# The opening of a two-block transformer kernel: filters, modulation, pooling and the first norm interleaved

## The reference, cut to what matters

```python
# first block
mod = silu(c) @ mod_w + mod_b             # 1024 -> 6 * 1024: sh1, sc1, g1, sh2, sc2, g2
hx = x * (1 + sc1) + sh1
p_g = centred_window_mean(hx_g, w) - hx_g # four groups of 256 channels, w = 2, 4, 8, 16
ox = (p_g @ pool_w_g) * pool_scale
x = layer_norm(ALPHA * x + g1 * ox, ...)
x = layer_norm(ALPHA * x + g2 * swiglu(x * (1 + sc2) + sh2), ...)
# second block: attention, FFN, and a long convolution whose filters come from a small sine network
h = sin(f * (z @ fw1 + b1)); h = sin(f * (h @ fw2 + b2)); h = sin(f * (h @ fw3 + b3))
filters = (h @ fw_out) * decay            # 2 orders, 2 directions, 1024 channels, 512 times
spectra = odd-frequency transform of their sums (cosine) and differences (sine)
```

## Time and profile before

| | |
|---|---|
| runs | 2045.27, 2048.11, 2051.75 us |
| profiled execution | 2047.33 us, span 2046.0 us |
| granted TensorE clock, mean | 0.932 of full speed |
| busy in the span | PE 1814.6 us (89%), DVE 1034.5 (51%), POOL 754.6 (37%), ACT 619.1 (30%) |
| moved | 193.97 MB, 95 GB/s in the mean |

### The profile page before, as it was taken

One profiled execution on the slowest core, in us unless ns is written; L12 is line 12 of the kernel. 1 busy time (PEld: TensorE's weight loads), 2 busy tenths in 40 slices (PEclk: granted clock), 3 DMA queues, 4 the chain that ended last, 5 costly groups with the idle time before them and its releaser, 6 DMA issues.

```text
span 2046.0 us, 19678 instructions
## 1 busy us (share of the span) xinstructions
PE 1814.6 (89%) x7816; PEld 1446.5 (71%) x7816; DVE 1034.5 (51%) x1494; ACT 619.1 (30%) x866; POOL 754.6 (37%) x348
## 2 busy tenths in 40 slices
PE   3882899999998899989999998999566889999997
PEld 1552688888877566768888886787555768888885
DVE  6998533332144758364444224523999464444224
ACT  1222322222224444243333213322222243333212
POOL 3123244444442310234444443342544324444442
PEclk9885799999998999989999998999778989999998
DMA  5771122323222100113232222422111312322232
GB/s 214 269 286 56 37 93 94 102 93 99 97 82 69 62 32 32 62 56 99 93 103 93 93 94 82 154 93 83 62 41 42 114 62 93 99 97 94 95 100 73
DMA packets 48148, 193.97 MB, mean 95 GB/s; under 512 B 5655, under 2 KB 5975, under 8 KB 43384
## 3 DMA queue, kind: packets, MB, share of 16 engines
q1 hardware_dynamic: 47480, 188.52, 27.2%
q10 hardware_dynamic: 576, 4.19, 0.5%
HBM read 180.11 MB, written 12.58 MB: 94 GB/s over the span
## 4 chain that ended last, share of the span: by engine, by line
PE 73%; DVE 19%; ACT 3%; POOL 2%; issue 2%; DMA 1%; ACTq 0%; SPq 0%; DVEq 0%
PE ps L414 23%; PE ps L415 23%; PE ps L416 23%; DVE mod_sums L1345 3%; POOL w_lo L1155 2%; PE ps L525 1%; DVE x_residual L1752 1%; DVE n_values L1477 1%; DVE filter_taps L1328 1%; DVE act_lo L1482 1%; PE ps L730 1%; DVE x_residual L1742 1%; ACT w_hi L854 1%; DVE x_residual L1744 1%; DVE hy_product_lo L1756 1%
## 5 line engine op out<-in xcount | busy, mean ns | idle before, releaser
L1155 POOL TENSOR_TENSOR w_lo<-w_raw,w_hi 128x1024 fp32r<-128x1024 f32 x258 | 621.9, 2411 | 984.7 <-ACT w_hi L854 984.7
L414 PE MATMUL ps<-act_hi,w_hi 128*128 128x512 f32 x1428 | 573.8, 402 | 74.0 <-POOL act_lo L1213 35.8
L415 PE MATMUL ps<-act_lo,w_hi 128*128 128x512 f32 x1428 | 566.9, 397 | 0.0
L416 PE MATMUL ps<-act_hi,w_lo 128*128 128x512 f32 x1428 | 566.0, 396 | 0.0
L854 ACT ACTIVATE w_hi<-w_raw 128x1024 fp32r<-128x1024 f32 x258 | 273.3, 1059 | 747.0 <-PE ps L416 736.1
L414 PEld LDWEIGHTS ps<-act_hi,w_hi 128*128 128x128 f32 x1428 | 274.4, 192 | 148.8 <-issue 51.4
L416 PEld LDWEIGHTS ps<-act_hi,w_lo 128*128 128x128 f32 x1428 | 274.8, 192 | 58.8
L415 PEld LDWEIGHTS ps<-act_lo,w_hi 128*128 128x128 f32 x1428 | 275.5, 193 | 56.3 <-issue 0.5
L414 PE MATMUL ps<-f_hidden_hi,w_hi 128*128 128x512 f32 x528 | 208.0, 394 | 1.9 <-POOL w_lo L1155 1.9
L415 PE MATMUL ps<-f_hidden_lo,w_hi 128*128 128x512 f32 x528 | 206.9, 392 | 0.0
L416 PE MATMUL ps<-f_hidden_hi,w_lo 128*128 128x512 f32 x528 | 206.6, 391 | 0.0
(11 more groups left out here) (263 smaller groups left out, 2296.6 us busy)
## 6 DMA issues: line engine op xcount, KB each, us to landing
w_raw<-in_w_stream SPq DMA_DIRECT2D x258, 512.0 KB, 3.7
mod_ring<-in_mod_w SPq DMA_DIRECT2D x16, 1536.0 KB, 10.2
hy_filter<-spectra SPq DMA_DIRECT2D x8, 1024.0 KB, 4.8
spectra<-filter_spectra SPq DMA_DIRECT2D x4, 1024.0 KB, 9.6
spectra<-filter_spectra ACTq DMA_DIRECT2D x4, 1024.0 KB, 7.4
decay<-in_decay SPq DMA_DIRECT2D x1, 2048.0 KB, 13.6
x_residual<-in_xT SPq DMA_DIRECT2D x8, 256.0 KB, 10.4
x_spill<-x_residual SPq DMA_DIRECT2D x8, 256.0 KB, 10.0
```

The source lines that it names most:

```text
L414: PE.matmul(o, lh, rh, start=start, stop=False, **kw)
L415: PE.matmul(o, lh, rl, start=False, stop=False, **kw)
L416: return PE.matmul(o, ll, rh, start=False, stop=stop, **kw)
L1155: GP.tensor_tensor(B.WL[:, c % 2, :], B.WR[:, c % 2, :], f32(B.WH[:, c % 2, :]), ALU.subtract).then_inc(S.w_lo, 1)
```

## The change

The four functions ahead of the first FFN become one, `start`, in each program, in which everything hangs on the eight filter units.

- Modulation in 48 tiles of 128x1024 (512 KB). Tiles 0 to 11 come with the input channels on the partitions, and PE makes each a column with eight fp32 products, four tiles before the second layer of the sine network, four before the third, four before the first taps. Tiles 12 to 47 come with the output channels on the partitions, and DVE multiplies each by a row of silu(c) and sums in one instruction, six tiles per unit. Four rings of 2, 5, 3 and 7 slots share seven buffers, four of which hold x in token order in between.
- Taps get four banks of their own hand-over: each tile has its own count of taps, decays, high and low parts. All low parts of the taps are POOL's. The order of the units becomes half, order, kind, and half of the decay table is loaded at a time.
- Pooling: PE multiplies x in token order with band matrices of 128x144 (unit 1), DVE forms the difference to hx before it is scaled by ALPHA, the linears come in units 2 and 3 in two banks, the mean in unit 4, the squares in unit 5, the inverse rows after unit 6, and the butterflies of unit 7 amid the normalisation.
- Spectra are stored after each unit from SP's queue. The loads of `fw_out`, the tables, the decay, x and the bands go to ACT's queue. The third and fourth chunk (up_1's base and base+1) are fetched after unit 4.

Buffers, new functions that only rename, and the host's layout are left out below.

```diff
+        own, shared = [self.MW[:, i, :] for i in range(3)], [self.x_tok[:, i, :] for i in range(4)]
+        self.mod_slots = (own[:2], own[2:] + shared, own, own + shared)
...
+MOD_ORDER = (1, 0, 2, 3, 4, 5)
+MOD_PE = 12
+MOD_BATCHES = (12, 18, 24, 30, 36, 42, 46, 48, 48)
+MOD_SLOTS = (2, 5, 3, 7)
+MOD_RINGS = (0, 12, 18, 24, 48)
+MOD_READS = (16, 24, 40, 48)
+MOD_COLUMN = 16
+BAND = P + 2 * PAD
+BAND_AT = (0, P - PAD, 2 * P - PAD, T - BAND)
+BAND_KIND = (0, 1, 1, 2)
+TAP_ORDER = (2, 3, 0, 1)
...
+def mod_place(t):
+    ring = sum(t >= first for first in MOD_RINGS[1:])
+    uses, slot = divmod(t - MOD_RINGS[ring], MOD_SLOTS[ring])
+    return ring, slot, uses
...
+    def mod_tiles(low, high):
+        for t in range(low, high):
+            ring, slot, uses = mod_place(t)
+            PE.wait_ge(S.mod_in[ring][slot], 16 * (uses + 1))
+            at = MOD_COLUMN + t
+            for k in range(KD):
+                ins = PE.matmul(ps[:, 7, at:at + 1], B.mod_slots[ring][slot][:, k * P:(k + 1) * P], B.sc[:, k:k + 1],
+                                start=(k == 0), stop=(k == KD - 1))
+            ins.then_inc(S.mod_pe, 1)
...
+    def taps(v):
+        n, order, kind = unit_parts(v)
+        for at, q in enumerate(TAP_ORDER):
+            if v:
+                PE.wait_ge(S.decayed, 4 * v - 3 + at)
+            PE.matmul(ps[:, q, :], B.hidn[:, q * P:(q + 1) * P], B.fsd[:, kind, order, n * 512:(n + 1) * 512],
+                      start=True, stop=True).then_inc(S.taps, 1)
...
+    def pool_windows():
+        PE.wait_ge(S.x_tok_in, 16)
+        PE.wait_ge(S.band_in, 16)
+        PE.wait_ge(S.mod_read, 1)
+        for k in range(KD):
+            if k == 1:
+                PE.wait_ge(S.odd_copied, 4)
+            if k >= 2:
+                PE.wait_ge(S.diff, k - 1)
+            for s in range(4):
+                ins = PE.matmul(ps[:, POOL_BANKS[k], BAND_AT[s]:BAND_AT[s] + BAND], B.x_tok[:, s, k * P:(k + 1) * P],
+                                B.band[:, 4 * BAND_KIND[s] + k // 2, :], start=(s == 0), stop=(s == 3),
+                                skip_group_check=True)
+            ins.then_inc(S.pooled, 1)
...
+    def pool_linear(cc, v):
+        wh, wl = chunk(cc)
+        for m in range(4):
+            tile = 4 * cc + m
+            if m < 2:
+                PE.wait_ge(S.diff, 8)
+                PE.wait_ge(S.odd_copied, 2 * v + 2)
+                if cc:
+                    PE.wait_ge(S.x_ready, 3 + m)
+            else:
+                PE.wait_ge(S.x_ready, tile - 1)
+            for k in range(2):
+                a = 2 * (m // 2) + k
+                PE.wait_ge(S.diff_lo, 4 * cc + a + 1)
...
+        PE.wait_ge(S.silu_c, 1)
+        mod_tiles(0, 4)
+        PE.wait_ge(S.consts_made, 5)
         for layer in range(2):
             PE.wait_ge(S.hid, layer + 1)
             PE.matmul(ps[0:HY_W, 0, :], B.fws[:, layer * HY_W:(layer + 1) * HY_W], B.hidn[0:HY_W, :],
                       start=True, stop=True).then_inc(S.mlp, 1)
...
+            mod_tiles(4 + 4 * layer, 8 + 4 * layer)
         PE.wait_ge(S.hid, 3)
-        PE.wait_ge(S.fw_sums, 2)
-        PE.wait_ge(S.consts_made, 5)
+        PE.wait_ge(S.fw_sums, 4)
         taps(0)
         for v in range(8):
             if v < 7:
                 taps(v + 1)
-            transforms(v)
-            mod_sum(2 * v)
...
+            for group in range(4):
+                if group == 0:
+                    if v == 2:
+                        PE.wait_ge(S.diff, 8)
+                    elif v in (3, 4):
+                        PE.wait_ge(S.x_ready, 4 * v - 8)
+                    elif v == 6:
+                        PE.wait_ge(S.ln_stat, 1)
+                transform(v, group)
+            if v == 1:
+                pool_windows()
+            elif v in (2, 3):
+                pool_linear(v - 2, v)
+            elif v == 4:
+                first_norm_mean()
+            elif v == 5:
+                first_norm_squares(v)
+            elif v == 6:
+                PE.wait_ge(S.decayed, 32)
+                inverse_rows_of(0, 3)
...
+        def filter_hi(v):
+            for at, q in enumerate(TAP_ORDER):
+                SC.wait_ge(S.decayed, 4 * v + at + 1)
+                if v:
+                    SC.wait_ge(S.spectrum, 4 * v - (1 if q < 2 else 0))
+                SC.activation(B.flh[:, q, :], B.flt[:, q, :], ACT.Copy).then_inc(S.flt_hi, 1)
+        def odd_part(v, f):
+            SC.wait_ge(S.spectrum, 4 * v + (1, 4)[f])
+            if v:
+                SC.wait_ge(S.bfly, 4 * v)
+            SC.activation(B.odd[:, f, :], ps[:, 5, :], ACT.Copy).then_inc(S.odd_copied, 1)
+        def pool_parts(cc):
+            for a in range(4):
+                k = 4 * cc + a
+                if cc == 0:
+                    SC.wait_ge(S.diff, k + 1)
+                    SC.activation(B.hx[:, k, :], B.hx[:, k, :], ACT.Identity,
+                                  bias=B.MOD[:, k:k + 1]).then_inc(S.diff_whole, 1)
+                else:
+                    SC.wait_ge(S.w_used, 1)
+                SC.wait_ge(S.diff_whole, k + 1)
+                SC.activation(AH[:, a, :], B.hx[:, k, :], ACT.Copy).then_inc(S.diff_hi, 1)
         for v in range(8):
-            for q in range(4):
-                SC.wait_ge(S.decayed, 4 * v + q + 1)
...
+            filter_hi(v)
+            if v == 1:
+                SC.wait_ge(S.x_in, 16 * KD)
+                SC.wait_ge(S.affine, 1)
+                SC.wait_ge(S.fw_sums, 4)
+                for k in range(KD):
+                    SC.activation(B.hx[:, k, :], X[:, k, :], ACT.Identity, bias=B.MOD[:, k:k + 1],
+                                  scale=B.AFF[:, 0, 0, k:k + 1]).then_inc(S.pool_in, 1)
+            odd_part(v, 0)
+            odd_part(v, 1)
+            if v == 1:
+                pool_parts(0)
+                for k in range(4, KD):
+                    SC.wait_ge(S.diff, k + 1)
+                    SC.activation(B.hx[:, k, :], B.hx[:, k, :], ACT.Identity,
+                                  bias=B.MOD[:, k:k + 1]).then_inc(S.diff_whole, 1)
+            elif v == 2:
+                for k in range(KD):
+                    SC.activation(X[:, k, :], X[:, k, :], ACT.Copy, scale=ALPHA_1).then_inc(S.x_scaled, 1)
+                pool_parts(1)
+            elif v == 4:
+                w_hi(2)
+                w_hi(3)
+            elif v == 5:
+                for k in range(KD):
+                    SC.wait_ge(S.ln_centred, k + 1)
+                    SC.activation(B.sq[:, k, :] if k < 4 else B.val[:, k, :], X[:, k, :],
+                                  ACT.Square).then_inc(S.ln_square, 1)
...
+        def filter_lo(v):
+            for at, q in enumerate(TAP_ORDER):
+                GP.wait_ge(S.flt_hi, 4 * v + at + 1)
+                GP.tensor_tensor(B.fll[:, q, :], B.flt[:, q, :], f32(B.flh[:, q, :]),
+                                 ALU.subtract).then_inc(S.flt_lo, 1)
+        def pool_lo(cc):
+            for a in range(4):
+                k = 4 * cc + a
+                GP.wait_ge(S.diff_hi, k + 1)
+                GP.tensor_tensor(B.AL[:, a, :], B.hx[:, k, :], f32(B.AH[:, a, :]),
+                                 ALU.subtract).then_inc(S.diff_lo, 1)
+        w_lo(0)
+        w_lo(1)
         for v in range(8):
-            for q in (0, 2):
-                GP.wait_ge(S.flt_hi, 4 * v + q + 1)
...
+            filter_lo(v)
+            if v in (1, 2):
+                pool_lo(v - 1)
+            elif v == 4:
+                w_lo(2)
+                w_lo(3)
+            elif v == 6:
+                norm(0)
...
+        def mod_tile(t):
+            m = 8 * MOD_ORDER[t // 8] + t % 8
+            ring, slot, uses = mod_place(t)
+            src = B.mod_slots[ring][slot]
+            VE.wait_ge(S.mod_in[ring][slot], 16 * (uses + 1))
+            VE.tensor_tensor_reduce(out=src, in0=src, in1=B.c_row[:, :], scale=1.0, scalar=0.0, op0=ALU.mult,
+                                    op1=ALU.add, accum_out=B.MOD[:, m:m + 1]).then_inc(S.mod_dve, 1)
...
+        decays(0)
+        mod_columns()
+        for v in range(7):
+            low, high = MOD_BATCHES[v], MOD_BATCHES[v + 1]
+            middle = min(low + 3, high)
+            mod_tiles(low, middle)
+            decays(v + 1)
+            mod_tiles(middle, high)
+            butterfly(v)
...
+            if v == 1:
+                for k in range(KD):
+                    VE.wait_ge(S.pooled, k + 1)
+                    VE.wait_ge(S.pool_in, k + 1)
+                    VE.scalar_tensor_tensor(out=B.hx[:, k, :], in0=ps[:, POOL_BANKS[k], :],
+                                            scalar=AFF[:, 0, 0, k:k + 1], in1=B.hx[:, k, :], op0=ALU.mult,
+                                            op1=ALU.subtract).then_inc(S.diff, 1)
+            elif v in (2, 3):
+                cc = v - 2
+                for m in range(4 * cc, 4 * cc + 4):
+                    if m % 4 == 3:
+                        VE.wait_ge(S.w_used, cc + 1)
+                    else:
```

(99 more changed lines are left out.)

462 lines of the change are left out of this document (132 added, 330 removed).

## The result

The changed kernel is slower: its runs have a median of 2071.8 us against 2049.93 us for the kernel before on the same chip, a ratio of 1.0086 (95% interval 1.005 to 1.0122). The forecast of 2021 us and its range up to 2048 us missed. The profiled execution took 2063.99 us for a span of 2062.7 us. Two of the four runs lie at 2064 us and two at 2079 us, with a granted clock of 0.942 and 0.934; I compare the profiled executions, which for both kernels are of the shorter kind, and the median holds some 8 us more.

A forecast was written before the change was run, and what follows sets the result against it. The opening was taken as bound by DVE, the 1793.1 us behind it as PE-busy and unchanged. The terms put the first plain linear at 226.1 instead of 252.9 us, 26.8 us less: forecast 2021 us, 8-in-10 range 1992 to 2048.

The forecast's parts named there:

- head, to the first decays: Start of the kernel with PE's twelve modulation tiles: first decays at 46.5 us, bounds 40 and 56.
- first decays, columns, unit 0: First decays and column copy 3 us, then the first filter unit 24 us, 10 of them a new wait.
- unit 1: Second filter unit, six modulation tiles on DVE: 15 us, before the band products.
- band products: Pooling products on PE in the second filter unit, 0.4 us each: DVE stands or works for 11 us.
- unit 4, mean: Fifth filter unit 15 us, then the mean on PE and centring on DVE, 10.6 us.
- unit 5: Sixth filter unit, with only four modulation tiles: 12 us, the squares counted apart at 10 us.
- unit 6: Seventh filter unit, with only two modulation tiles: 9 us.
- tail: From the seventh unit's butterflies to the first plain linear, with the last unit and normalisation: 28 us.
- Head starves: Rival, chance 0.05: twelve tiles through two slots at 5 us each, first taps at 62 rather than 46, 2036 us.
- The tile at twice the price: Rival, chance 0.13: DVE's multiply-and-reduce takes twice 1.25 us in 36 instructions, 45 us more, 2066 us.
- Contention with POOL: Filter units: DVE's two-input instructions wait for POOL, three waits of 0.8 to 1 us, making a unit 15 us.
- The rest: Everything from the first plain linear to the end: 1793.1 us, carried over unchanged.

The follow-up runs named there:

- a2_warm: The changed kernel with 24 unused fp32 products of 128 columns on PE ahead of the first modulation tile: 2077.92 us in one run.
- a4_dve_head: The changed kernel with all 48 modulation tiles on DVE, none on PE, and a first ring of seven slots: 2045.6 us median, ratio 0.9975.
- a1_small_first: The changed kernel with the bulk loads on ACT's queue waiting until the small tensors have landed: 2073.04 us median, ratio 1.0102.
- a3_fetch_early: The changed kernel with weight chunks 0 and 1 fetched behind modulation tile 11 instead of tile 19: 2056.73 us median, ratio 1.0033.
- a6: The changed kernel with the edits of a1_small_first, a3_fetch_early, a4_dve_head and a5 together: 2023.03 us median, ratio 0.9869.
- a8: The changed kernel with two of the four taps' low parts per unit given back to DVE in units 0 to 6: 2072.58 us, ratio 1.008.
- a7: The kernel of a6 with two of the four taps' low parts per unit given back to DVE in units 0 to 6: 2027.08 us median, ratio 0.9861.
- a5: The changed kernel with the high and low parts of chunks 2 and 3 made in unit 6, later than before: 2064.98 us in one run.

## Why the prediction was wrong

The sum was 226.1 us for the start of the first plain linear; it is 265.4. Term by term, measured less predicted:

| step | predicted | measured | error |
|---|---|---|---|
| head, to the first decays | 46.5 | 68.3 | +21.8 |
| first decays, columns, unit 0 | 27 | 31.5 | +4.5 |
| unit 1 | 15 | 18.6 | +3.6 |
| band products | 11 | 9.7 | -1.3 |
| units 2 and 3, linears | 42 | 43.3 | +1.3 |
| unit 4, mean | 25.6 | 19.9 | -5.7 |
| unit 5 | 12 | 18.2 | +6.2 |
| squares | 10 | 10.8 | +0.8 |
| unit 6 | 9 | 13.3 | +4.3 |
| tail | 28 | 31.7 | +3.7 |

**The step that failed** is the head: "2.0 us a tile ... partly at half clock ..., which is 2.9 a tile" and "I let the first land at about 10 us". The tile takes 3.47 us, the first starts at 17.39, and the twelve with two small layers between them and 3 us of waits end at 66.0. That is 68.3 against an upper bound of 56, more than half of the whole error, and by itself it turns 27 us of gain into 5. Of its 21.8 us 7.4 are the late first tile, 12.6 the twelve tiles with what stands between them (the two small layers take 3.8 us on PE, which I had put in the shadow), and 1.8 the first taps. The price of 1.50 us for six products came from a stretch in which PE had just worked on the transforms, and the pooling stretch showed a clock of 0.54 where PE did little. The bound of such a tile is 8 x 0.25 x 2 = 4.0 us, not 2.9, and the measured 3.47 lies between. The record of the clock could not warn me, for it reads 1.00 in the head of the kernel before too, but the durations there could:
```profile
4.22 1.96 PE L447 MATMUL ps<-positions_features,fw 33*64 33x512 f32 x2 [4.22 <-DMA fw_bias_freq<-in_hy_small]
43.49 3.70 PE L459 MATMUL ps<-fw_out_sum_diff,filter_hidden 128*128 128x512 f32 x8 [2.74 <-DVE filter_taps L1328]
```
A record of 512 columns takes 0.98 us in the head and 0.46 us behind it, so the kernel before has the lower level in its head as well. a2_warm shows the two prices side by side and a4_dve_head what the choice of PE costs: 20 us.

The landing of the first tile was the smaller half of that step. I had 3 MB of filter loads beside it; the small tensors came at 12.70 instead of 4.22 us and the tile at 17.3. Yet a1_small_first, which puts this right, gains 1 us: the second and third tile then wait 4.22 and 2.58 us for their transfers, and the early start is lost again.

- *Head starves* (chance 0.05) named the stage and nearly the hour, first taps at 62; they came at 66. Its mechanism was mostly another: it had 5 us a tile for want of transfers, while 3.47 us a tile are PE's own work and the waits for transfers sum to 3 us. I had the price of starving and not that of the clock.
- *Unit 0* was seen (ACT with chunks 0 and 1 ahead of the taps, the fetch behind tile 17, "19 us until DVE can add"), and the term of 27 us was 4.5 short. 2.1 of it are in the first decays and the copy (68.29 to 73.42 us instead of 3 us: eight records of the first taps take 6.36 us), 1.4 in the chunk, which lands 7.4 us behind DVE's first tile instead of 6. I costed a wait of 10 us and did not ask what lifts it; a3_fetch_early shows 12.9 us.
- *The tile at twice the price* (0.13) had the right sign of the whole and the wrong cause. The instruction takes 1.22 us and 1.15 from start to start, as taken from the earlier trace rows. Two fp32 operands from SBUF with an accumulator cost no double here. The rule of the Trainium skill that the prediction cited (Vector Engine (DVE) Microarchitecture Reference, Points that are easy to get wrong) is stated for the scalar-tensor-tensor form, and the trace names this instruction CUSTOM_DVE_ANT_0, with a read of the accumulator of 0.08 us behind it; whether the rule holds for its own form with an accumulator no run shows.
- *Contention with POOL* was sized rightly in kind, wrongly in place. Alone a tile is 1.22 us, beside POOL mostly 2.27 and up to 3.35, so DVE loses 1.1 to 2.1 us by each. By the rule of the Trainium skill (SBUF — State Buffer, Who interferes with whom) the one that comes second waits for the whole of the other's instruction. The trace agrees: the losses lie between nothing and the length of one POOL instruction, 1.27 us for a low part of the taps and 2.33 us for a w_lo. But it costs most in unit 5, where w_lo of two chunks and four low parts run in a row: I let 2 us stay of that step because "the mean covers most", and it was 8.8: ACT has chunk 2 only at 189.40 us, after the mean's product, which ends at 186.5. Units 2 and 4, of 15 us in the forecast, took 14.7 and 12.7; unit 3 took 19.4, against 15 and 3 for the queue on POOL.
- *Unit 1* waited 4.8 us for tiles, while x in token order (2 MB) stands in the same queue (DMA share 0.93 in its row above), which I had costed at nothing. That it is x which delays them is not tested.
- *The band products* came to 0.27 to 0.34 us a product where I took 0.4. *Mean* was shorter than forecast (7.2 against 10.6), because PE's product starts at 179.51 us and runs beside DVE's last tiles and butterflies of unit 4: DVE waits 2.40 us for it, and I had 5.7. *Unit 6* and the *tail* were 4.3 and 3.7 us longer than forecast; no run takes them apart, and their cause stays open.
- *The rest* is 4.2 us longer in this profile, which was one of the forecast's own signs of being wrong. It is 1797.3 to 1798.4 us in the profiles of a3, a4, a6 and a8, 1795.5 in a7, and 1808.7 to 1809.0 in those of a1, a2 and a5, where the granted clock between 764.5 and 814.5 us is 0.70 to 0.81. The 4.2 us are a sum of pieces of either sign; over the sixteen chunks that lie between 524 and 612 us in the kernel before it grows by 1.5 us with a clock of 1.00 in both kernels. Why is open; I had carried it over unchanged.

## What to carry to other kernels

Price a product by the clock that the engine will have in that place. Here PE was at its lower level in the head of both kernels, even while it was busy for 45 of 49 us with one-column products, so the half-clock price was the one to take, and PE was three times slower than DVE with the same tile (3.47 against 1.15 us). Read the level of a stretch off a known product there. When work is woven together, look at the first hand-over of each queue (here a fetch behind eight tiles): what the first unit lost stayed lost, 12.9 us by the order of one queue. Read a stage off the chain of waits, but test a shortening of it before you count it: half of POOL's low parts in seven units could be taken away without any gain.

## What the hardware showed unexpectedly

- In the head the record of the granted clock says 1.00 while products run at the lower level: 0.434 us a product at "1.00" in the changed kernel's head, the same 0.437 us at a recorded 0.50 in a2_warm, and 0.227 us just behind its burst. The duration of a known product is the surer clock.
- Small tensors on one queue were held up by bulk on another: the first product waits until 12.70 us with 3 MB on ACT's queue beside it, and until 4.64 once that bulk waits for them (4.22 in the kernel before).
- A DVE tile with both inputs in SBUF took up to 3.35 us beside POOL, 2.7 times its price alone, more than the doubling of the earlier trace rows; the POOL instruction beside it was a w_lo of 2.33 us.
